# Query weights of heads 6 and 7 kept from tile 0 to tile 1, mixer pieces through one buffer, and the second gathered row named early

## The reference

```python
q = (xt @ w_query).reshape(T, PEER_HEADS, 2, PEER_KEY_DIM // 2)      # 8 heads, two halves of 128
s = einsum('thcd,hckd->thck', q, sub_keys)                           # 128 keys for each half
s_top, i_top = top_k(s, 16)
cand = s_top[..., 0, :, None] + s_top[..., 1, None, :]               # 16 x 16 sums
g_s, g_pos = top_k(cand, 16)
e_idx = take(i_top[..., 0, :, None] * 128 + i_top[..., 1, None, :], g_pos)
h = gelu(einsum('td,thkd->thk', x, expert_u[e_idx]))
y = einsum('thk,thkd->td', softmax(g_s) * h, expert_v[e_idx])
```

## Time and profile before

| | |
|---|---|
| device time, median of 3 runs | 940.52 us (939.14 to 941.0) |
| the profiled execution: its own device time | 939.81 us |
| its span, first to last instruction | 937.9 us |
| busy: PE, DVE, ACT, POOL | 81%, 64%, 46%, 32% of the span |
| moved by DMA | 339.54 MB, of which gathers 268.45 MB |

### The profile page before, as it was taken

One profiled execution on the slowest core, in us unless ns is written; L12 is line 12 of the kernel. 1 busy time (PEld: TensorE's weight loads), 2 busy tenths in 40 slices (PEclk: granted clock), 3 DMA queues, 4 the chain that ended last, 5 costly groups with the idle time before them and its releaser, 6 DMA issues.

```text
span 937.9 us, 11751 instructions
## 1 busy us (share of the span) xinstructions
PE 757.0 (81%) x4032; PEld 347.8 (37%) x4032; DVE 599.6 (64%) x1437; ACT 430.8 (46%) x1184; POOL 299.6 (32%) x295
## 2 busy tenths in 40 slices
PE   8999999999879989889675787777766777676664
PEld 6886665655624544443121433232311111111110
DVE  1622853546698969686657565786667666677445
ACT  1143315422579888764334434364443434434333
POOL 0010031002334536434233334343533334333430
PEclk9999999999968979989796857687967656566676
DMA  7634555548999999999999999999999999999993
GB/s 272 257 122 172 226 199 194 223 180 313 424 422 388 423 420 418 423 419 422 424 423 420 422 419 423 420 420 423 421 419 421 421 421 421 421 420 422 419 421 143
DMA packets 46140, 339.54 MB, mean 362 GB/s; under 512 B 6112, under 2 KB 6144, under 8 KB 9216
## 3 DMA queue, kind: packets, MB, share of 16 engines
q0 software_dynamic: 37152, 268.45, 69.2%
q1 hardware_dynamic: 8928, 70.34, 19.1%
HBM read 337.70 MB, written 1.06 MB: 361 GB/s over the span
## 4 chain that ended last, share of the span: by engine, by line
DMA 46%; PE 35%; ACT 8%; DVE 7%; issue 3%; POOL 1%; DVEq 0%; SPq 0%; ACTq 0%; POOLq 0%
DMA late<-in_uv,eidx 30%; DMA ring<-in_uv,eidx 15%; PE ps L721 6%; PE ps L1129 6%; PE ps L745 6%; PE ps L912 4%; PE ps L869 4%; ACT late L1178 4%; ACT L1178 3%; DVE late L1930 2%; DVE ring L1930 2%; PE ps L728 1%; PE ps L737 1%; ACT tmp L1178 1%; PE ps L809 1%
## 5 line engine op out<-in xcount | busy, mean ns | idle before, releaser
L1178 ACT ACTIVATE late<-late 128x1 f32<-128x1 f32 (+3 forms) x787 | 222.1, 285 | 330.3 <-DVE late L1930 312.0
L1129 PE MATMUL ps<-ring,late 64*64 64x512 f32 x928 | 167.5, 810 | 76.9 <-ACT late L1178 76.7
L1129 PE MATMUL ps<-late 64*64 64x512 f32 x960 | 164.9, 783 | 73.3 <-ACT late L1178 73.0
L2029 POOL DMA_INDIRECT late<-in_uv,eidx x118 | 128.9, 1093 | 233.9 <-PE ps L1129 173.7
L1930 DVE CUSTOM_DVE_ANT_0 late<-late,x_sb 128x1024 f32<-128x1024 f32 x120 | 146.9, 1225 | 84.1 <-DMA late<-in_uv,eidx 83.7
L1930 DVE CUSTOM_DVE_ANT_0 ring<-ring,x_sb 128x1024 f32<-128x1024 f32 x116 | 142.1, 1225 | 85.7 <-DMA ring<-in_uv,eidx 85.0
L2029 POOL DMA_INDIRECT ring<-in_uv,eidx x116 | 126.6, 1091 | 192.9 <-PE ps L1129 181.4
L1178 ACT ACT_TABLE_LOAD x85 | 109.1, 1283 | 27.2 <-PE ps L737 14.6
L1129 PEld LDWEIGHTS ps<-late 64*64 64x64 f32 x960 | 31.9, 158 | 181.8 <-ACT late L1178 163.9
L1129 PEld LDWEIGHTS ps<-ring,late 64*64 64x64 f32 x928 | 30.3, 160 | 178.4 <-ACT late L1178 164.5
L1178 ACT ACTIVATE tmp<-ps 128x512 f32<-128x512 f32 (+4 forms) x79 | 38.8, 499 | 65.0 <-PE ps L721 41.2
(11 more groups left out here) (267 smaller groups left out, 769.7 us busy)
## 6 DMA issues: line engine op xcount, KB each, us to landing
wring<-in_wts SPq DMA_DIRECT2D x21, 2048.0 KB, 11.6
ring<-in_wts SPq DMA_DIRECT2D x2, 2048.0 KB, 8.8
wring<-in_wts SPq DMA_DIRECT2D x2, 1428.0 KB, 5.8
wring<-in_wts SPq DMA_DIRECT2D x2, 1388.0 KB, 6.3
ring<-decay_sums SPq DMA_DIRECT2D x2, 1024.0 KB, 5.8
lnw<-in_ln SPq DMA_DIRECT2D x4, 512.0 KB, 12.2
late<-in_uv,eidx POOLq DMA_INDIRECT x118, 16.9
ring<-in_uv,eidx POOLq DMA_INDIRECT x116, 16.9
```

Source lines behind the costliest of these rows:

```text
L1129: last = mm(o[t][n * HD:(n + 1) * HD, :], factor[tokens, :], values[tokens, n * 512:(n + 1) * 512], start=start, stop=stop, skip_group_che ...
L1178: return nc.scalar.activation(out, in_, func, **kw)
L2029: G.indirect_dma_start(row(slots[g]), None, uv, bass.IndirectOffsetOnAxis(eidx[:, u % 2, k:k + 1], 0)).then_inc(row_here[slots[g]], 16)
```

## The change

**Query weights.** Piece 3 of the query weights belongs to heads 6 and 7. It is the last that tile 0 loads. Tile 1 now begins with these heads (`QUERIES[1]` has the piece order 3, 0, 1, 2) and takes them from the buffer that still holds the piece. Its second load is gone: 27 pieces instead of 28.

**Buffers.** Because piece 19 stays in buffer 1 until tile 1's first query product, pieces 20 to 24 (the four mixer pieces and the next query piece) all go through buffer 0. A load then waits until PE has used the piece directly before it.

**Table.** The first transposes `mT` move from step 60 to 57 and the mixer parts from 64, 67, 69, 71, 77, 79, 81, 83 to 61, 63, 68, 70, 77, 78, 84, 86. Residual, norm, `hT` and the first query product come one step later.

**Second row.** The second best sum of a head is either best key of half 0 with second key of half 1 or the other way round. DVE copies the numbers of the two best keys of each half (`leaders`). POOL adds the two rival sums; DVE compares them; POOL works out both expert numbers, selects one and gathers row 1 without waiting for the sort.

```diff
-QUERIES = [[... 7 groups of tile 0 ...], [(n, 0, 2) for n in range(4)]]
+QUERIES = [[... the same ...], [(n, 0, 2) for n in (3, 0, 1, 2)]]
+KEPT = 3
...
-    put("pe", 60, "mT", 0)
-    put("dve", 63, "mT", 0)
-    for part, k in enumerate((64, 67, 69, 71)):
+    put("pe", 57, "mT", 0)
+    put("dve", 60, "mT", 0)
+    for part, k in enumerate((61, 63, 68, 70)):
...
-    for part, k in enumerate((77, 79, 81, 83)):
+    for part, k in enumerate((77, 78, 84, 86)):
...
+        kept_at = len(pieces) - 3 - 4 - 1
+        homes = [n % WSLOTS for n in range(kept_at + 1)]
+        homes += [1 - homes[kept_at]] * 5 + [homes[kept_at], 1 - homes[kept_at]]
...
-                    end = pieces[k - WSLOTS][2]
+                    end = pieces[piece_behind(k)][2]
...
+                    if (i, piece) == (1, KEPT):
+                        query[0] = kept[0]
...
+                step(V.tensor_copy(leaders, topi[:, :, 0:2]))
+                V.scalar_tensor_tensor(eidx[:, 0, 0:1], leaders[:, 0, 0:1], float(NKEY), leaders[:, 1, 0:1], ALU.mult, ALU.add).then_inc(idx_ready, 1)
+                dve.wait_ge(rivals_ready, 1)
+                tt(ahead, rivals[:, 0:1], rivals[:, 1:2], ALU.is_ge).then_inc(ahead_ready, 1)
...
+            def second_expert():
+                link(G.tensor_scalar(scaled, leaders[:, 0, :], float(NKEY), None, ALU.mult))
+                for n in range(2):
+                    last = G.tensor_tensor(experts_of[:, n:n + 1], scaled[:, n:n + 1], leaders[:, 1, 1 - n:2 - n], ALU.add)
+                link(last)
+                link(G.tensor_tensor(apart_by, experts_of[:, 0:1], experts_of[:, 1:2], ALU.subtract))
+                pool.wait_ge(ahead_ready, 1)
+                link(G.tensor_tensor(apart_by, apart_by, ahead, ALU.mult))
+                link(G.tensor_tensor(apart_by, apart_by, experts_of[:, 1:2], ALU.add))
+                link(G.tensor_copy(eidx[:, 0, 1:2], apart_by))
+
+            pool.wait_ge(first_step, 2)
+            for n in range(2):
+                last = G.tensor_tensor(rivals[:, n:n + 1], top[:, 0, n:n + 1], top[:, 1, 1 - n:2 - n], ALU.add)
+            last.then_inc(rivals_ready, 1)
```

More of the change, by code:

```diff
@@ L79 @@
 NU = [NH // 2, NH]
-QUERIES = [[(0, 0, 1), (0, 1, 1), (1, 0, 2), (2, 0, 1), (2, 1, 1), (3, 0, 1), (3, 1, 1)], [(n, 0, 2) for n in range(4)]]
+QUERIES = [[(0, 0, 1), (0, 1, 1), (1, 0, 2), (2, 0, 1), (2, 1, 1), (3, 0, 1), (3, 1, 1)], [(n, 0, 2) for n in (3, 0, 1, 2)]]
+KEPT = 3
 EARLY = 3
@@ L444, in layer @@
         gsm = view(kv_place[0] + 192, 4, src=late)
+        leaders = view(kv_place[0] + 204, 2, 2, src=late)
+        rivals = view(kv_place[0] + 208, 2, src=late)
+        experts_of = view(kv_place[0] + 210, 2, src=late)
+        scaled = view(kv_place[0] + 214, 2, src=late)
+        ahead = view(kv_place[0] + 212, 1, src=late)
+        apart_by = view(kv_place[0] + 213, 1, src=late)
         numbers = view(kv_place[0] + 196, APART, src=late)
@@ L560, in group_of @@
             groups = QUERIES[u // PH]
-            return next(g for g, (piece, first, heads) in enumerate(groups) if 2 * piece + first <= u % PH < 2 * piece + first + heads)
+            ends = itertools.accumulate(heads for _, _, heads in groups)
+            return next(g for g, end in enumerate(ends) if u % PH < end)
         def await_full(eng, *name):
@@ L608, in layer, with piece_behind @@
             order += [(14 + n, (2 * i + 1, ("mixS", i, 1), 2 * i + 2, ("mixA", i, 1))[n]) for n in range(4)]
-            order += [(18 + n, ("q", i, max(g for g, group in enumerate(QUERIES[i]) if group[0] == n))) for n in range(4)]
+            order += [(18 + n, ("q", 1, 0) if n == KEPT else ("q", i, max(g for g, group in enumerate(QUERIES[i]) if group[0] == n)))
+                      for n in range(4) if (i, n) != (1, KEPT)]
         pieces = [(shapes[w], starts[w], end) for w, end in order]
         piece_no = iter(range(len(pieces)))
+        kept_at = len(pieces) - 3 - 4 - 1
+        homes = [n % WSLOTS for n in range(kept_at + 1)]
+        homes += [1 - homes[kept_at]] * 5 + [homes[kept_at], 1 - homes[kept_at]]
+        loads = [sum(homes[n] == homes[m] for n in range(1, m + 1)) for m in range(len(pieces))]
+        def piece_behind(k):
+            return max(n for n in range(k) if homes[n] == homes[k])
         def piece_view(k):
             (kind, *dims), _, _ = pieces[k]
-            at = (k % WSLOTS) * WPIECE
+            at = homes[k] * WPIECE
             v = wring[:, at:at + math.prod(dims)]
@@ L703, in next_piece @@
                 if k:
[L704 removed]
+                    pe.wait_ge(w_here[homes[k]], 16 * loads[k])
                 return piece_view(k)
@@ L903, in query_part @@
                             await_taken(pe, "hT", i, half)
-                    if first == 0:
+                    if (i, piece) == (1, KEPT):
+                        query[0] = kept[0]
+                    elif first == 0:
                         query[0] = next_piece()
+                        if piece == KEPT:
+                            kept[0] = query[0]
                     query[1] = await_free(pe, "q", i, n)
@@ L1343, in key_scores_copy @@
                 o = await_full(act, "s", i, n)
-                place_of = (i * PH + 2 * piece + first) * 2 * NKEY
+                place_of = (i * PH + sum(group[2] for group in QUERIES[i][:n])) * 2 * NKEY
                 taken(f(s_all[:, place_of:place_of + heads * 256], o[:, 0:heads * 256], ACT.Copy), "s", i, n)
@@ L1769, in experts @@
                     step(V.tensor_reduce(eij[:, :, half], cells, AX, ALU.add))
-                    rest = slice(max(a, 1), b)
+                    rest = slice(max(a, 2), b)
                     V.scalar_tensor_tensor(eidx[:, 0, rest], eij[:, 0, rest], float(NKEY), eij[:, 1, rest], ALU.mult, ALU.add).then_inc(idx_ready, 1)
```

31 lines of the change are left out of this document (17 added, 14 removed).

## The result

The changed kernel takes 933.35 us (median of 5 runs, 932.52 to 935.82) against 940.0 us for the kernel before (5 runs, 939.14 to 941.0): a ratio of 0.9934, 95% interval 0.9921 to 0.9947, which is 6.2 us less of 940. The forecast was 935.5 us. Its profiled execution took 933.35 us, with a span of 931.5 against 937.9.

The account below looks back on a forecast made before the run. The second stage was taken to be bound by DMA bytes at about 421 GB/s. Terms: saved load -5.0, second row 0, mixer 0, sum -5.0 us, giving 935.5 us on the median; range 932.6 to 938.8 us.

Parts of the forecast that it names:

- The saved load, -5.0: Tile 1's second load of piece 3, 2.097 MB at 421 GB/s, comes off the end: -5.0 us, bounds 0 and 5.0.
- POOL's chain: Six dependent small POOL operations between gathers 0 and 1 take 1.8 us, so gather 1 goes out at about 224.7.
- rival 5: POOL's new operations are slow and delay gather 0 and, through DVE's wait, the sort: 937.1 us, chance 0.04.
- The second row, 0: The queue's lead of 2.5 us from the earlier gather 1 doesn't reach the end: 0, bounds -2.2 and 0.
- From there to about 300 us each request waits for PE, so the requests go out at the same times: From row 8's request at 249.91 us, requests keep their times and the queue is empty 2.5 us longer.
- the 7.8 us taken for an unqueued landing: Row 24, issued at 295.17, needed 7.8 us and was taken not to be behind a queue.
- rival 1: The lead of the second row stays, a further -2.2 us: 933.3 us, chance 0.18.
- The mixer through one buffer, 0: PE stands 0 to 5.2 us at step 68 for a weight load, covered by the queue: 0, bounds 0 and +4.
- The cover of 8.5 us: At the mixer, 8.5 us may go before DMA is empty, from gathers landing 21.3 us after issue.
- The margin of 0.3 us: What is left of the mixer's queue after moved parts use up to 3 us and the stall 5.2.
- dip of "about 2.5 us" deeper: Sign of being right: the windows of 285 to 306 us emptier by about 2.5 us.
- rival 2: DMA runs empty 1.5 to 4 us at steps 60 to 72 because PE is late: 938.2 us, chance 0.14.

Follow-up runs that it names:

- e1: The changed kernel with the second row chosen as before, from the sort, the rest kept: 934.46 us, ratio 0.9947 to the kernel before.
- e3: The kernel before with the four mixer pieces through one buffer and the new table steps, all 28 loads kept: 939.99 us, ratio 1.0001.
- e4: The changed kernel without the load of the last query piece (heads 4 and 5 of tile 1): 928.43 us, ratio 0.9878 to the kernel before.
- e5: The changed kernel with the load of piece 19 held back until row 15 is used: 937.54 us, ratio 0.9973 to the kernel before.
- e2: The kernel before with only the second row chosen early, nothing else changed: 937.74 us, ratio 0.9975.
- e7: The changed kernel with the table steps of the kernel before, all mixer pieces through one buffer: 942.31 us, ratio 1.0026 to the kernel before.
- e6: The kernel before with the load of piece 19 held back until row 15 is used, nothing else: 942.41 us, ratio 1.0024.
- e8: The kernel before with the load of piece 19 held back only until row 3 is used: 940.91 us, ratio 1.0017.
- e9: The changed kernel with the load of piece 19 held back only until row 3 is used: 935.44 us, ratio 0.9952 to the kernel before.
- e10: The changed kernel with three small DVE operations moved behind row 9's dot instead of ahead of it: 933.24 us, ratio 0.9931 to the kernel before.

## Why the prediction was right, and where it wasn't

**Bounds and rate: right.** Bytes at 421 GB/s set the second stage, after as before.

**The saved load, -5.0: right.** e1 measured -5.0 with the buffers and the steps in it, which by themselves cost +0.1 (e3); e4 measured another -5.3.

**POOL's chain: right.** 2.0 us for 1.8, gather 1 at 225.02 for 224.7; gather 0 at 221.58, 0.2 us later than before. The delay of rival 5 didn't occur.

**The second row, 0: wrong in size, and in the step behind it.** The step that failed is "From there to about 300 us each request waits for PE, so the requests go out at the same times". The requests wait for PE, but PE waits for ACT, ACT for DVE's dots, and two of these had waited for landings, at 256 and 261 us, just ahead of the stretch of the earlier trace rows. The lead took these waits away, and the requests of rows 18 and 24 moved by 1.5 and 2.2 us. The second fault is the 7.8 us taken for an unqueued landing: those of e5 took 5.7 to 6.1. Nor was row 24's landing set by its issue: in after it was issued 2.2 us earlier, landed 1.2 us earlier (301.73 for 302.97), and again 4.4 us behind row 23. It measured -2.35 alone (e2) and -1.2 on top of the load (e1 to after). This is rival 1's result (933.3 us) by a way that the prediction didn't give; the range held the time because it took rival 1 in, not because this step was right. That the two parts, -5.0 and -2.35, don't add up to -6.2 lies within their intervals (each 0.0009 to 0.0015 of 940, up to 1.4 us), so whether they hinder each other stays open. Open too is why row 8 landed 12.3 us after its issue in e1 and 11.4 in before.

**The mixer through one buffer, 0: right in the sum, half right in the way.** PE's parts, in the timeline of after:

```profile
411.51 3.60 PE L888 MATMUL ps<-wring,tmp 128*128 128x512 f32 x8
426.62 5.36 PE L888 MATMUL ps<-wring,tmp 128*128 128x512 f32 x8 [4.41 <-DMA wring<-in_wts]
...
460.20 3.70 PE L888 MATMUL ps<-wring,tmp 128*128 128x512 f32 x8
476.82 5.86 PE L888 MATMUL ps<-wring,tmp 128*128 128x512 f32 x8 [6.28 <-DMA wring<-in_wts]
```

At step 68 PE comes 7.1 us after the part of step 63 ends (7.5 forecast) and stands 4.41 us (0 to 5.2). At step 84 no wait was forecast, since six steps were taken at a gather's time each; but after the heavy parts PE is behind its rows, takes the six steps in 6.6 us, and waits 6.28 us for a load of 12.9. The cover of 8.5 us was about right: waits up to 6.9 us cost nothing (e3), one of 8.35 opened a hole (e7). Behind both waits the part ran in part at the 1.2 GHz level (granted clock 0.60 at 426 to 429 us, 0.50 at 476.8 to 479), 5.4 and 5.9 us for 3.6, which the bound held. The margin of 0.3 us was counted too close: no window behind the stall dips. Perhaps the stall and the moved steps don't use up the queue in one place; no run shows it.

**The rest.** Of the dip of "about 2.5 us" deeper, 0.5 came; the "dip at 395 to 450 us" that would have spoken for rival 2 didn't. The range of 932.6 to 938.8 held the time, near its lower end.

## What to carry over

When a queue is the bound, ask of every wait for its landings whether the engine that waits also sets the next requests; look for such waits ahead of the stretch in which the queue runs low, not in it. A load that is held back for the sake of a more urgent one leaves a hole where it was taken out if nothing else can be queued there (1.2 to 3.3 us at 232 to 264 us in e5, e6, e8 and e9), and held for long it opens another one behind it (e5, e6). Price a change by bytes, and by the empty time of DMA summed over windows: here this account met twelve measured changes to within 1.4 us.

## What the hardware showed beyond the forecast

A lone gather of 1 MB lands in 5.6 us, and rows 8, 20 and 21 of e5 in 5.7 to 6.1. PE's mixer part runs 3.60 to 3.70 us at 2.4 GHz, and 5.1 to 6.8 us when it comes first after a wait for weights of 3.2 to 9.5 us; the next one is at 3.70 again. The part at 453.85 us of after took 5.39 us without a wait before it (granted clock 0.50 at 453 to 456 us), so the wait isn't the only way to the lower level. In e10 moving DVE's work by 1.2 us moved a stretch of PE at 1.2 GHz onto the path that sets the requests; whether that took the whole gain isn't shown. In before, after and e2 row 24 lands 4.4, 4.4 and 3.5 us after the row ahead of it, 1 to 2 us beyond a row's 2.49; which of the waits around 295 us makes this wasn't separated.
